# A decoder layer pair and a vision block in float32: the first attention's output product from seven block products in place of eight

## The reference

```python
o = causal_block_attention(q_nope, q_rope, k_nope, k_rope, v).reshape(B, L, MLA_V_W)
return (o * jax.nn.silu(z)) @ w_out       # (512 x 2048) @ (2048 x 1024)
...
h = h + rmsnorm(y, post_norm[layer])
return h[:, N_META:]
```

## Time and profile before

| | us |
|---|---|
| median of 3 timed runs | 2503.44 |
| lowest and highest | 2501.28, 2508.81 |
| the profiled execution | 2494.57 |
| its span in the trace | 2492.8 |
| TensorE busy in the span | 2286.7 (92%) |
| VectorE busy | 961.1 (39%) |
| ScalarE busy | 747.1 (30%) |
| matmuls of the output product (L736), 256 passes | 111.2 |

### The profile page before, as it was taken

How to read it: one execution, slowest core, us unless ns; L and a number is a source line. 1 busy time by engine, 2 the same in 40 slices (tenths; PEclk the granted TensorE clock), 3 DMA queues, 4 the chain that set the end, 5 groups by cost and what they waited for, 6 DMA issues and landing times.

```text
span 2492.8 us, 42870 instructions
## 1 busy us (share of the span) xinstructions
PE 2286.7 (92%) x19147; PEld 1651.8 (66%) x19147; DVE 961.1 (39%) x1821; ACT 747.1 (30%) x1376; POOL 0.2 (0%) x4
## 2 busy tenths in 40 slices
PE   4899999999998998788999999798999988999999
PEld 4678778878777687444444444356566546888888
DVE  1435535544544301222322220356226634556532
ACT  2434343343443201233433421442344422000000
POOL 0000000000000000000000000000000000000000
PEclk8899989989999799889998999899999998999999
DMA  4122222122121142111111112121110031433330
GB/s 160 35 69 71 68 69 70 52 87 70 52 70 52 49 118 68 30 30 30 30 46 57 37 34 68 55 70 36 35 34 1 1 101 34 131 85 89 94 101 26
DMA packets 200624, 150.41 MB, mean 60 GB/s; under 512 B 16360, under 2 KB 198122, under 8 KB 200058
## 3 DMA queue, kind: packets, MB, share of 16 engines
q1 hardware_dynamic: 200442, 147.69, 19.9%
HBM read 143.41 MB, written 4.26 MB: 59 GB/s over the span
## 4 chain that ended last, share of the span: by engine, by line
PE 85%; ACT 6%; DVE 5%; issue 3%; SPq 1%; DMA 1%; DVEq 0%; ACTq 0%
PE PS L2226 15%; PE PS L1505 11%; PE PS L1533 5%; PE PS L442 5%; PE PS L674 5%; PE PS L736 4%; PE PS L1286 3%; PE PS L1295 3%; PE PS L1288 3%; PE PS L1465 2%; PE PS L792 2%; PE PS L680 1%; PE PS L717 1%; PE PS L718 1%; PE PS L2347 1%
## 5 line engine op out<-in xcount | busy, mean ns | idle before, releaser
L2226 PE MATMUL PS<-hn_all,ring 128*128 128x264 f32 x1536 | 426.3, 414 | 2.5 <-DVE scr L2781 1.5
L2226 PEld LDWEIGHTS PS<-hn_all,ring 128*128 128x128 f32 x1536 | 292.5, 201 | 51.2 <-ACT scr L2551 1.9
L674 PE MATMUL PS<-hn_all,ring 128*128 128x512 f32 x256 | 117.0, 601 | 7.3 <-DMA ring<-in_mla_w_q_up 7.3
L442 PE MATMUL PS<-big,ring 128*128 128x264 f32 x512 | 115.8, 390 | 2.4 <-DMA ring<-in_gdn_w_out 2.4
L442 PEld LDWEIGHTS PS<-big,ring 128*128 128x128 f32 x512 | 98.3, 192 | 19.9 <-issue 2.7
L736 PE MATMUL PS<-big,ring 128*128 128x512 f32 x256 | 111.2, 592 | 0.0
L1286 PE MATMUL PS<-ring,hn_all 128*128 128x256 f32 x384 | 95.4, 403 | 2.5 <-ACT scr L1731 2.5
L1505 PE MATMUL PS<-scr 128*128 128x256 f32 x352 | 84.8, 384 | 4.6 <-DVE scr L1996 4.6
L674 PEld LDWEIGHTS PS<-hn_all,ring 128*128 128x128 f32 x256 | 48.2, 193 | 59.6 <-issue 47.5
L736 PEld LDWEIGHTS PS<-big,ring 128*128 128x128 f32 x256 | 48.2, 190 | 58.3 <-issue 57.7
L869 ACT ACTIVATE scr<-PS,scr 128x528 f32<-128x528 f32 (+1 forms) x64 | 34.6, 541 | 169.6 <-DVE scr L955 169.4
(11 more groups left out here) (471 smaller groups left out, 4043.1 us busy)
## 6 DMA issues: line engine op xcount, KB each, us to landing
ring<-in_w_mod SPq DMA_DIRECT2D x24, 1024.0 KB, 5.4
ring<-in_gdn_w_in SPq DMA_DIRECT2D x16, 1024.0 KB, 5.5
ring<-in_w_in SPq DMA_DIRECT2D x12, 1024.0 KB, 5.4
hn_all<-in_w_ffn_in SPq DMA_DIRECT2D x22, 512.0 KB, 5.3
ring<-in_w_ffn_in SPq DMA_DIRECT2D x22, 512.0 KB, 5.2
ring<-in_mla_w_in SPq DMA_DIRECT2D x9, 1024.0 KB, 5.5
ring<-in_gdn_w_in SPq DMA_DIRECT2D x16, 512.0 KB, 5.3
ring<-in_gdn_w_out SPq DMA_DIRECT2D x8, 1024.0 KB, 7.2
```

The source lines that it names most:

```text
L442: ins = nc.tensor.matmul(PS[:, 2 * (m % 2) + h, 0:x.stop - x.start], wslot(m % 4, P, 16)[:, k, :], src[:, k, x], start=(k == 0), stop=(k = ...
L674: ins = mm(o, wz_pair(p)[:, k, j * P:(j + 1) * P], hq[:, k, :], start=(k == 0), stop=(k == KD - 1))
L2226: ins = mm(o, wslot(slot_, 256)[:, k, m * P:(m + 1) * P], hn[:, k, b * HALF:(b + 1) * HALF], start=(k == 0), stop=(k == KD - 1))
```

## The change

The product is split in 2 x 2 blocks: the features in heads 0 to 7 and 8 to 15, the tokens in 0 to 255 and 256 to 511, the output in pairs of tiles (unit u = 0 to 3 makes tiles 2u and 2u+1). Of weights A11, A12, A21, A22 (8 heads x 128 columns each; the first index is the tile, the second the half of the features, as `m_w_of` gives them) and four blocks of `oq`, seven products of 8 matmuls with 256 columns are made in place of eight. For that come
- four token sums T1 to T4, each 8 heads x 256 tokens, made head by head by `token_sums(n)`: for heads 8 to 14 VectorE does this one head later, ahead of its wait for the value matmuls, for head 15 behind its multiply. T1 is written over the second half of heads 0 to 7;
- four weight sums S1 to S4 of 8 x 128 columns in each unit (`weight_sums`);
- seven output sums in each unit on VectorE (`block_sums`), which read PSUM and write `yq` and two buffers, and one copy of product 1 on ScalarE (`m_p1`). ScalarE's copies of whole tiles go, and its squares read `yq` instead of PSUM.

PSUM banks are four (7, 1, 0, 4), each half filled. The weights come in four loads of 2 MB. The context's tokens are loaded to another place (`hn_all`), and the square of the context has a buffer of its own (`sq2c`); their sizes stay.

The diff, cut to its core (the rest renames semaphores and the buffers of the context):

```diff
-        def gemm_out_dve(dve, n, gain, y, h, width):
+        def gemm_out_dve(dve, n, gain, y, h, width, sums=None):
...
+            def added(m):
                 dve.wait_ge(*up(n + "o_sq", m + 1))
...
                     ins = nc.vector.tensor_tensor(acc_, acc_, gsqb[m % 2][:, 0:width], ALU.add)
                 ins.then_inc(s[n + "o_acc"], 1)
+            if sums:
+                sums(added)
+            else:
+                for m in range(KD):
+                    added(m)
+                dve.wait_ge(*up(n + "out_ev", KD))
             dve.wait_ge(*up(n + "o_rstd", 1))
-            dve.wait_ge(*up(n + "out_ev", KD))
...
+        MHALF = SEQ // 2
+        MOUT = (7, 1, 0, 4)
+        m_W = [ring[:, b * PAIR:(b + 1) * PAIR].rearrange("p (k n) -> p k n", k=16) for b in range(2)]
+        m_S = [scr[:, 4 * L + 2 * D + k * D:4 * L + 2 * D + (k + 1) * D].rearrange("p (k n) -> p k n", k=8) for k in range(4)]
+        m_T = [oq[:, 0:8, MHALF:SEQ]] + [scr[:, 10624 + k * 2 * D:10624 + (k + 1) * 2 * D].rearrange("p (k n) -> p k n", k=8)
+                                         for k in range(3)]
+        m_p1, m_v, m_w = (scr[:, 16768 + k * MHALF:16768 + (k + 1) * MHALF] for k in range(3))
+        def m_w_of(u):
+            w = m_W[u % 2]
+            return w[:, 0:8, 0:P], w[:, 8:16, 0:P], w[:, 0:8, P:2 * P], w[:, 8:16, P:2 * P]
...
             wv = t["mla_w_out"][0].rearrange("(k p) n -> p k n", p=P)
-            for k in range(8):
-                if k % 2 == 0 and k < 4:
-                    sp.wait_ge(*up("pj", last_piece(13) if k == 0 else len(PIECES)))
-                if k >= 4:
-                    sp.wait_ge(*up("mout", k - 3))
-                sp.dma_start(wslot(k % 4, P, 16), wv[:, :, k * P:(k + 1) * P]).then_inc(s["mo%d" % (k % 4)], 16)
+            for u, free in enumerate((up("pj", last_piece(13)), up("pj", len(PIECES)), up("mout", 7), up("mout", 14))):
+                sp.wait_ge(*free)
+                sp.dma_start(m_W[u % 2], wv[:, :, 2 * u * P:2 * (u + 1) * P]).then_inc(s["mo%d" % (u % 2)], 16)
...
-            def out_rows(m, ks):
+            def out_product(q, a, b, ks=range(8)):
                 for k in ks:
-                    ins = mm(PS[:, MOUT[m % 2], :], wslot(m % 4, P, 16)[:, k, :], oq[:, k, :], start=(k == 0), stop=(k == 15))
-                if ks[-1] == 15:
+                    ins = mm(PS[:, MOUT[q], 0:MHALF], a[:, k, :], b[:, k, :], start=(k == 0), stop=(k == 7))
+                if ks[-1] == 7:
                     ins.then_inc(s["mout"], 1)
-            def early(m, a, b):
+            def early(a, b):
                 if a == 0:
-                    pe.wait_ge(*up("mo%d" % m, 16))
-                    if m == 0:
-                        pe.wait_ge(*up("pev", len(PIECES)))
-                    else:
-                        pe.wait_ge(*up("ex", order_no(15, 0)))
-                out_rows(m, range(a, b))
+                    pe.wait_ge(*up("mo0", 16))
+                    pe.wait_ge(*up("pev", len(PIECES)))
+                out_product(0, m_w_of(0)[0], oq[:, 0:8, 0:MHALF], range(a, b))
             for n in range(MLA_HEADS):
                 nxt = n + 1 < MLA_HEADS
...
                 if nxt:
                     piece(n + 1, "z", 0)
                 else:
-                    early(0, 0, 4)
+                    early(0, 4)
                 score(n, 1)
                 turn(n, 3)
                 if nxt:
                     piece(n + 1, "z", 1)
                 else:
-                    early(0, 4, 8)
+                    early(4, 8)
                 score(n, 0)
                 turn(n, 2)
                 if nxt:
                     piece(n + 1, "qn")
-                else:
-                    early(0, 8, 11)
                 turn(n, 1)
                 if nxt:
                     piece(n + 1, "qr")
                     piece(n + 1, "ka")
-                else:
-                    early(0, 11, 14)
                 turn(n, 0)
-                if not nxt:
-                    early(1, 0, 4)
                 if nxt:
                     piece(n + 1, "kb")
                     if n % 2 == 1:
...
                 ins.then_inc(s["pv"], 1)
-            out_rows(1, range(4, 14))
             pe.wait_ge(*up("ogm", MLA_HEADS))
-            out_rows(0, range(14, 16))
-            out_rows(1, range(14, 16))
-            for m in range(2, KD):
-                pe.wait_ge(*up("mo%d" % (m % 4), 16 * (m // 4 + 1)))
-                pe.wait_ge(*up("mo_sq", m - 1))
-                out_rows(m, range(16))
-                if m == 3:
+            pe.wait_ge(*up("ex", order_no(15, 0)))
+            for u in range(KD // 2):
+                A11, A12, A21, A22 = m_w_of(u)
+                S1, S2, S3, S4 = m_S
+                T1, T2, T3, T4 = m_T
+                pe.wait_ge(*up("mo%d" % (u % 2), 16 * (u // 2 + 1)))
+                if u > 0:
+                    pe.wait_ge(*up("mv_d", 7 * u - 2))
+                    out_product(0, A11, oq[:, 0:8, 0:MHALF])
+                    pe.wait_ge(*up("mv_d", 7 * u - 1))
+                out_product(1, A12, oq[:, 8:16, 0:MHALF])
+                if u == 2:
                     pe.wait_ge(*up("cx_in", 16 * NCTX))
                     for n in range(NCTX):
                         for k in range(KD):
                             ins = nc.tensor.transpose(PS[:, CTX_BANK[n] + k // 4, (k % 4) * P:(k % 4 + 1) * P],
                                                       xcin[:, n, k * P:(k + 1) * P], ident)
                         ins.then_inc(s["cx_tr"], 1)
-                if m == 6:
+                if u == 3:
                     pe.wait_ge(*up("sq2_d", 1))
                     for k in range(KD):
-                        ins = mm(PS[:, 2, 0:CTX], const("mean_d"), sq2[:, k, 0:CTX], start=(k == 0), stop=(k == KD - 1))
+                        ins = mm(PS[:, 2, 0:CTX], const("mean_d"), sq2c[:, k, :], start=(k == 0), stop=(k == KD - 1))
                     ins.then_inc(s["ms2"], 1)
+                if u > 0:
+                    pe.wait_ge(*up("mv_d", 7 * u))
+                pe.wait_ge(*up("mtp_d", 32))
+                pe.wait_ge(*up("msu_d", 4 * u + 2))
+                out_product(2, S2, T2)
+                out_product(3, S1, T1)
+                pe.wait_ge(*up("mp_d", u + 1))
+                pe.wait_ge(*up("msu_d", 4 * u + 4))
+                out_product(0, S3, T3)
+                pe.wait_ge(*up("mv_d", 7 * u + 1))
+                out_product(1, S4, oq[:, 8:16, MHALF:SEQ])
+                pe.wait_ge(*up("mv_d", 7 * u + 2))
+                out_product(2, A22, T4)
             pe.wait_ge(*up("mo_acc", KD))
             mm(PS[:, 4, 0:SEQ], const("mean_d"), gacc[:, 0:SEQ], start=True, stop=True).then_inc(s["mo_ms"], 1)
...
-            def context(m):
-                if m == 4:
+            def squared(m):
+                act.wait_ge(*up("mv_d", 7 * (m // 2) + 6 + m % 2))
+                if m >= 2:
+                    act.wait_ge(*up("mo_acc", m - 1))
+                A(gsqb[m % 2][:, 0:SEQ], yq[:, m, :], ACT.Square).then_inc(s["mo_sq"], 1)
+            for u in range(KD // 2):
+                act.wait_ge(*up("mout", 7 * u + 1))
+                if u > 0:
+                    act.wait_ge(*up("mv_d", 7 * u - 5))
+                A(m_p1, PS[:, MOUT[0], 0:MHALF], ACT.Copy).then_inc(s["mp_d"], 1)
+                if u > 0:
+                    squared(2 * u - 2)
+                    squared(2 * u - 1)
+                if u == 2:
                     for n in range(NCTX):
                         act.wait_ge(*up("cx_tr", n + 1))
                         ins = A(ctxT[:, :, n * P:(n + 1) * P],
                                 PS[:, CTX_BANK[n]:CTX_BANK[n] + 2, :].rearrange("p b (k n) -> p (b k) n", n=P), ACT.Copy)
                     link(ins)
-                if m == 5:
-                    A(sq2[:, :, 0:CTX], ctxT, ACT.Square).then_inc(s["sq2_d"], 1)
-            gemm_out_act(act, "m", yq, lambda ap: ap[:, 0:SEQ], lambda b: PS[:, {0: MOUT[0], 2: MOUT[1], 4: 4}[b], :], context)
+                    A(sq2c, ctxT, ACT.Square).then_inc(s["sq2_d"], 1)
+            squared(KD - 2)
+            squared(KD - 1)
+            act.wait_ge(*up("mo_ms", 1))
+            act_link(A(grs[:, 0:SEQ], PS[:, 4, :], ACT.Ln, bias=eps))
+            A(grs, grs, ACT.Exp, scale=-0.5).then_inc(s["mo_rstd"], 1)
...
+            def token_sums(n):
+                k, at = n - 8, 4 * (n - 8)
+                T1, T2, T3, T4 = (x[:, k, :] for x in m_T)
+                h0, h1 = oq[:, n, 0:MHALF], oq[:, n, MHALF:SEQ]
+                dve.wait_ge(*up("ogm", n + 1))
+                V.tensor_tensor(T3, h1, T1, ALU.subtract).then_inc(s["mtp_d"], 1)
+                dve.wait_ge(*up("mtp_d", at + 1))
+                V.tensor_tensor(T1, T1, oq[:, k, 0:MHALF], ALU.subtract).then_inc(s["mtp_d"], 1)
+                dve.wait_ge(*up("mtp_d", at + 2))
+                V.tensor_tensor(T2, h1, T1, ALU.subtract).then_inc(s["mtp_d"], 1)
+                dve.wait_ge(*up("mtp_d", at + 3))
```

(68 more changed lines are left out.)

3 lines of the change are left out of this document (2 added, 1 removed).

## The result

| | us |
|---|---|
| changed kernel, median of 5 runs | 2489.83 (2484.07 to 2493.63) |
| kernel before, median of 5 runs | 2503.61 (2501.28 to 2508.81) |
| ratio | 0.9939, 95% interval 0.992 to 0.9959 |
| profiled execution, before and after | 2494.57 and 2489.83 |
| span, before and after | 2492.8 and 2488.0 |

The two profiled executions are only 4.7 us apart. So the first question is not what the change did but which of these differences is the change.

A forecast was written before the change was run, and what follows sets the result against it. TensorE alone bounds the product's stretch. Of 13.2 us saved in passes, 3.1 go to the bare head 15 and 0.8 to sums: 9.3; less 1.7 for a clock fall, 7.6, so 2495.8 us from 2503.44; range 2490 to 2502.5.

The forecast's parts named there:

- Which time: Whole kernel: the same difference comes off profiled run and timed median 2503.44, giving 2487.0 and 2495.8 us.
- The passes: Output product on TensorE: 256 long passes (109.9 us) become 448 short ones at 0.2159 us (96.7), 13.2 us less.
- The bare head and the new wait: Head 15 with few early matmuls, then VectorE's sums: bulk starts 8.95 us earlier; 3.1 and 0.8 us lost.
- The wait before product 3: Unit 0: TensorE waits 0.8 us for VectorE's four token sums and two weight sums.
- The end and the units: Last pass to averaging matmul 1.9 us against 1.88, nothing gained; VectorE's queue in later units costs nothing, cover 4.4 us.
- The loads: Four 2 MB weight loads, taken to land in 11.4 us against 19.5 us until wanted; cover 8 us.
- The clock: Head 15's pauses more often than not halve TensorE's clock; short fall costs 1.7 us, long one 5.8 us.
- one short fall: Likeliest case, chance 0.45: clock halved 3.4 us at head 15, costing 1.7; gain 7.6 us, time 2495.8.
- The forecast of 7.6 us: Whole kernel: stage gain of 9.3 us less 1.7 us for one short clock fall.
- theory B: Experiments' rival for the measured 13.8 us: the change also saves about 4 us outside its stage; no chance given.
- The rivals: No fall 2494.1 us (0.26); long fall 2499.9 (0.17); waits in units 2499 (0.06); late loads, 2511 at 32 us (0.06).
- No wait for VectorE or for weights in units 1 to 3: Sign: a TensorE wait there, or heads 9 to 15 longer than before, would show the forecast wrong.

The follow-up runs named there:

- e5: Changed kernel plus an eighth, unused product of the same size in each unit; 2505.59 us, ratio 1.0015 to the kernel before.
- e3: Changed kernel with the first two weight sums of unit 0 made before head 14's multiply, in their own buffer; 2490.34 us.
- e4: e3 plus seven matmuls of product 2 and seven of unit 1's product 1 moved into head 15's pauses; 2486.50 us, ratio 0.9947 to the kernel before.
- e2: Changed kernel again, no edit, beside the kernel before; 2494.23 us, ratio 0.9981.
- e6: Changed kernel with token sums made in four 2048-column operations behind head 15's multiply, not head by head; 2496.33 us, ratio 0.9981 to the kernel before.
- e9: Changed kernel a third time, no edit; 2492.59 us, ratio 0.9961 to the kernel before.
- e11: Changed kernel once more, no edit, for one more profile; stage (first value matmul of head 14 to averaging matmul) 122.28 us.
- e1: Kernel before, unchanged, timed against itself; 2501.24 us against 2501.43, ratio 1.0002.
- e8: The kernel of e4 run again, no further edit; 2484.80 us, ratio 0.9932 to the kernel before.
- e12: The kernel of e4 once more, no edit, for one more profile; stage (first value matmul of head 14 to averaging matmul) 116.97 us.
- e10: Changed kernel plus six 256-column matmuls with unused results in head 15's pauses; 2488.28 us, ratio 0.9946 to the kernel before.
- e7: Kernel before with no output-product matmuls inside head 15, all behind the multiply; 2506.97 us, ratio 1.0025 to the kernel before.
- The filled kernel: The kernel of e4, e8 and e12: early weight sums and product matmuls moved into head 15's pauses; medians 2486.50 and 2484.80 us.

## Why the prediction failed

The mechanism held, and the step that failed is "Which time", with the lower end of the range that is built on it: I took the gain of one stage off a median of three runs (2503.44) and let the median of the changed kernel lie only 4 us low. The scatter of such medians is the term that was too small: of the medians of five drawn from all runs of the changed kernel, a quarter lie below 2490, the end of the range.

- **The passes.** 448 at 0.2159 us, in the bulk without a pause. Right, and e5 shows the price of a product by itself.
- **The bare head and the new wait.** The retimed chain had the value matmuls 15.0 us after those of head 14; they came after 14.86. The bulk of the product was to start 8.95 us earlier. Counted from head 14, product 2 starts after 19.12 us against 28.24 of the first bulk pass before: 9.12. The wait before product 3 was to cost 0.8 us; it shows as 0.60 of idle time, and e3 gets 0.8 back. Beside the passes 3.8 us were lost, 0.8 to the sums and 3.0 to the bare head; I had 0.8 and 3.1. e3 and e4 show both by taking them away.
- **The end and the units.** 1582.26 to 1584.15 is 1.89 us against 1.88, and VectorE's queue held nothing up. The loads landed in 7.9 us, not 11.4 (below): twice the bytes did not take twice the time, and this cover was larger than I said.
- **The clock.** I put the chance of one short fall at 0.45 and priced it at 1.7 us. The first profile of the changed kernel had none; the three others of the same kernel all had it, at 1.66 us. So the case that I named likeliest is the common one, though the first profile was of the other, and the pauses draw it: six of the seven profiles with these pauses in head 15 (after, e2, e3, e5, e6, e9, e11) have a fall there, none of the six where matmuls fill them (before, e1, e4, e8, e12, e10) has, and of these e10 differs from the changed kernel by six idle matmuls alone. e7, whose head is barer still, has one of 6.8 us. The pauses alone don't decide it, since the first profile had them without a fall; its earlier falls lie elsewhere too (below). What the Trainium skill says in "TensorE: Matmul & The Clock Gate", section "Part 1: The HAM clock gate (the "warmup" mystery)", that the clock follows how busy TensorE has lately been, these runs bear out: 60% busy ahead of the fall of e2, by pauses of which none is longer than 1.2 us.
- **The size.** Taken together, the runs of the kernel before that the comparisons use (86, without those of e1) have a median of 2501.8 us and those of the changed kernel (30) 2492.4: 9.4 us, 95% interval 6.1 to 12.1 by resampling; by the means 8.7 (6.2 to 11.2). The forecast of 7.6 us lies in both, and so does the 9.34 of the stage. 13.8 does not. Drawing 5 and 5 from these runs gives 13.7 us or more in 15% of the cases. I had read the spread from three runs of the kernel before (7.5 us) while 33 spread over 31. Of the 6.0 us between my time and the measured one, 1.6 are the median that I started from (2503.44 for 2501.8), 1.8 the gain (9.4 for 7.6), and 2.6 the five runs measured (2489.83 for 2492.4).
- **What stays open.** Whether the runs of the changed kernel lose 1.7 us to the fall as often as its profiles say can't be read off medians with this scatter. That the medians' 9.4 lies above 9.34 - 1.7 = 7.6 is not significant. Nor do they rule theory B out: 7.6 with 4 us more elsewhere is 11.6, still inside the interval.
- **The rivals.** No wait for VectorE or for weights in units 1 to 3, heads 9 to 15 at their 22.9 and 27.6 us. No run shows theory B, and none excludes it for certain.

The filled kernel beats both: 17 runs with a median of 2485.0 us, by the means 14.1 us (10.9 to 17.0) faster than the kernel before and 5.4 (1.8 to 8.8) faster than the changed one, where its stage gives 3.6 and the missing fall up to 1.7.

## What to carry to other kernels

When a product gets shorter, look at what its matmuls covered: here 3.8 of 13.1 us went back, because the work that had filled the last head's chain was cut from 15.45 to 3.45 us and sums were put behind it, and a few matmuls moved back into its pauses, with two sums made earlier, returned 3.6 of the 3.8. Judge a gain of 0.3% by the stage in the trace and by dozens of runs; a median of five can be 5 us off. Pauses of half a microsecond to a microsecond close to one another can cost a second time through the clock.

## What the runs showed of the hardware

The eight loads of 1 MB had runs of 512 bytes and landed in 5.7 us; the four of 2 MB have runs of 1 KB and landed in 7.9, 265 GB/s in place of 184. It is the size of the load more than the length of the runs: three loads of another weight in the changed kernel have 1 MB and runs of 1 KB, and landed in 5.5:

```profile
ring<-in_mla_w_out SPq DMA_DIRECT2D x4, 2048.0 KB, 7.9
ring<-in_mla_w_in SPq DMA_DIRECT2D x3, 1024.0 KB, 5.5
```

Ahead of the stage, the falls of the clock stand at the same places of the program in most profiles: the one of 13.7 us begins 133.6 to 133.8 us ahead of the value matmuls of head 14 in eleven of the fourteen profiles (1327.8 and 1461.53 in the kernel before, 1336.7 and 1470.31 in e2). In the first profile of the changed kernel it is two heads earlier, and that is the one execution of this kernel without a fall in head 15:

```profile
1279.30:1293.00 13.70, 12.33 (x23) 6.14 (x24) 0.69 (x1) 1.57 (x3) 0.00 (x0) 0.50 0.00 0
```

So these executions differ less by a fall here and there than by a whole pattern of them. That a handful of runs shares one pattern would explain the first five, but only one of the five was profiled: it is not shown.
